# Second mixer of a fused decoder: the panels of the differential values ahead of the dilated queries and keys, and twelve half panels with the dilated rotary turns spread among the heads

## The reference

```
cq, ck, cv, dq, dk, dv = split_cols(h @ w_in, IN1_SPLITS)          # six times 512 columns
cq = apply_rope(cq, cos128, sin128) * DIL_DH ** -0.5               # dilated: 4 heads of 128
ck = apply_rope(ck, cos128, sin128)
o_c = dilated_attention(cq, ck, cv)
q1, q2 = apply_rope(dq[..., 0, :], ...), apply_rope(dq[..., 1, :], ...)   # differential: 4 heads, 2 x 64
k1, k2 = apply_rope(dk[..., 0, :], ...), apply_rope(dk[..., 1, :], ...)
o_d = differential_attention(q1, q2, k1, k2, dv, lam)              # softmax 1 - lam * softmax 2, times dv
o_d = rmsnorm(o_d, diff_norm) * (1.0 - lambda_init)
return concatenate([o_c, o_d]) @ w_out
```

## Time and profile before

| | |
|---|---|
| median of three runs | 1557.31 us |
| span of the profiled execution | 1554.0 us |
| what lies around the span, against that median | 3.3 us |
| PE busy | 1499.8 us, 97% |
| DVE busy | 1171.7 us, 75% |
| ACT busy | 763.9 us, 49% |
| chain that ended last: PE | 76% |
| chain that ended last: DVE, ACT | 13%, 7% |
| the mixer's stretch, from the first differential swap to the first matmul of `out1` | 778.81 to 861.12 us |

### The profile page before, as it was taken

One profiled execution on the slowest core, in us unless ns is written; L12 is line 12 of the kernel. 1 busy time (PEld: TensorE's weight loads), 2 busy tenths in 40 slices (PEclk: granted clock), 3 DMA queues, 4 the chain that ended last, 5 costly groups with the idle time before them and its releaser, 6 DMA issues.

```text
span 1554.0 us, 23910 instructions
## 1 busy us (share of the span) xinstructions
PE 1499.8 (97%) x9958; PEld 1343.8 (86%) x9958; DVE 1171.7 (75%) x1387; ACT 763.9 (49%) x935; POOL 94.1 (6%) x66
## 2 busy tenths in 40 slices
PE   7999999999999999999998899999999989999988
PEld 6888899988888888888887888888899869899967
DVE  7878668756887788787676688787779676579774
ACT  5333456445433453334445543345565675564662
POOL 2000010011000010000100100001113001003100
PEclk9999999999999999999999999999999999999999
DMA  7555535214655555555441365554344315444302
GB/s 272 209 190 189 170 131 188 82 55 159 213 189 199 179 178 190 190 185 194 163 163 56 134 216 190 192 188 175 151 163 152 109 42 189 175 149 152 120 28 81
DMA packets 51888, 246.76 MB, mean 159 GB/s; under 512 B 4619, under 2 KB 5771, under 8 KB 27718
## 3 DMA queue, kind: packets, MB, share of 16 engines
q1 hardware_dynamic: 50662, 238.29, 43.8%
q0 software_dynamic: 1120, 6.96, 1.2%
HBM read 244.18 MB, written 1.05 MB: 158 GB/s over the span
## 4 chain that ended last, share of the span: by engine, by line
PE 76%; DVE 13%; ACT 7%; issue 3%; DMA 0%; SPq 0%; DVEq 0%; ACTq 0%; POOL 0%
PE ps L1109 20%; PE ps L1111 10%; PE ps L1060 9%; PE ps L1062 9%; PE ps L1061 9%; PE ps L1162 8%; PE ps L1317 4%; PE ps L1163 4%; DVE w_lo L1890 3%; ACT w_hi L1571 2%; DVE act_two L1998 1%; PE ps L1465 1%; ACT work L1784 1%; ACT act_two L1649 1%; PE ps L1454 1%
## 5 line engine op out<-in xcount | busy, mean ns | idle before, releaser
L1571 ACT ACTIVATE w_hi<-raw 128x2048 fp32r<-128x2048 f32 x186 | 355.2, 1914 | 396.6 <-PE ps L1111 276.6
L1890 DVE TENSOR_TENSOR w_lo<-raw,w_hi 128x2048 fp32r<-128x2048 f32 x186 | 432.4, 2331 | 139.1 <-ACT w_hi L1571 136.3
L1109 PE MATMUL ps<-act_two,w_hi 128*128 128x512 f32 x1408 | 445.1, 398 | 5.0 <-DVE w_lo L1890 2.4
L1060 PE MATMUL ps<-act_two,w_hi 128*128 128x256 f32 x1120 | 329.0, 294 | 9.9 <-DVE act_two L1998 5.3
L1111 PEld LDWEIGHTS ps<-act_two,w_lo 128*128 128x128 f32 x1408 | 265.6, 189 | 63.1
L1061 PE MATMUL ps<-act_two,w_hi 128*128 128x256 f32 x1120 | 316.7, 283 | 0.0
L1062 PE MATMUL ps<-act_two,w_lo 128*128 128x256 f32 x1120 | 316.7, 283 | 0.0
L1111 PE MATMUL ps<-act_two,w_lo 128*128 128x256 f32 x1408 | 277.5, 279 | 0.0
L1060 PEld LDWEIGHTS ps<-act_two,w_hi 128*128 128x128 f32 x1120 | 214.6, 192 | 17.0 <-issue 6.1
L1109 PEld LDWEIGHTS ps<-act_two,w_hi 128*128 128x128 f32 x1408 | 215.5, 190 | 8.0 <-DVE w_lo L1890 3.6
L1061 PEld LDWEIGHTS ps<-act_two,w_hi 128*128 128x128 f32 x1120 | 214.7, 192 | 4.4 <-issue 4.3
(11 more groups left out here) (286 smaller groups left out, 1995.5 us busy)
## 6 DMA issues: line engine op xcount, KB each, us to landing
raw<-panels SPq DMA_DIRECT2D x184, 1024.0 KB, 4.8
raw<-panels SPq DMA_DIRECT2D x80, 512.0 KB, 4.9
raw<-panels SPq DMA_DIRECT2D x8, 256.0 KB, 5.7
table<-tab POOLq DMA_DIRECT2D x1, 1472.0 KB, 9.4
table<-tab POOLq DMA_DIRECT2D x1, 1216.0 KB, 5.5
xn<-x_in SPq DMA_DIRECT2D x4, 256.0 KB, 4.9
work<-mem_in POOLq DMA_DIRECT2D x1, 1024.0 KB, 9.3
xn<-mem_in POOLq DMA_DIRECT2D x1, 1024.0 KB, 6.3
```

The lines of the kernel that those rows point to most:

```text
L1060: pe.matmul(o, l[0], r[0], start=start, stop=False, skip_group_check=shared)
L1109: pe.matmul(grid(ps[:, bank + half], 2), w[half][0], act_two[:, slots[c]], start=c == 0, stop=False)
L1571: nc.scalar.activation(w_hi[:, s], raw[:, s], ACT.Copy).then_inc(panel_hi, 1)
L1890: tt(w_lo[:, s], raw[:, s], w_hi[:, s].bitcast(F32), ALU.subtract).then_inc(panel_lo, 1)
```

## The change

Four things change, all in the order of `in1` and its neighbours:

1. The two panels of the differential v come as panels 4 and 5, the dilated q and k as panels 6 to 9. The array of panels in memory stays as it was; SP takes them by a list, `IN1_SOURCE`. Transfers keep their number and size.
2. Only panels 4 and 5 stand whole among the differential turns. Their places become 0 and 2, so two swaps stand between them. Panels 6 to 11 are woven in as twelve halves, and two more splits are made by halves.
3. The four dilated turns move from two pairs (before the first and before the second head's scores) to rounds 1 and 2 (one each) and round 3 (two). They all use bank 3, so each swap waits for the rope just before it. Bank 3 was the second bank of `turn_p`; the differential heads now all turn in bank 2, and each of these waits for the copy of the head before.
4. The copy of panel 9 stands right behind its second half. The copies of the others stay behind the following round.

The last places of `BESIDE_1` are 4 and 5 for panel 11 before, and 5 and 6 after.

```
+AT_ONCE = [("act", "evacuate", ("in1", 9))]
...
             out.append(first)
+            if rest and rest[0] in AT_ONCE:
+                out.append(rest.pop(0))
...
-BESIDE_1 = [0, 0, 1, 1, 2, 3, 4, 5]
+BESIDE_1 = [0, 0, 0, 1, 1, 1, 2, 2, 3, 4, 5, 6]
+IN1_SOURCE = [0, 1, 2, 3, 8, 9, 4, 5, 6, 7, 10, 11]
...
-    out += weave(rounds(ROPE, [("r64b", g) for g in (0, 2, 1, 3)]), panel_list("in1", None, 4, 8), range(4))
-    ropes = [[(e, k, (("r128", g),)) for g in pair for e, k, _ in ROPE] for pair in ((0, 2), (1, 3))]
+    out += weave(rounds(ROPE, [("r64b", g) for g in (0, 2, 1, 3)]), panel_list("in1", None, 4, 6), [0, 2])
+    turns = [[]] + [[(e, k, (("r128", g),)) for e, k, _ in ROPE] for g in (0, 1)] + [[(e, k, (("r128", g),)) for g in (2, 3) for e, k, _ in ROPE]]
...
-    out += weave(merge(ropes, heads, [[]] * 7 + norms, [[]] * 9 + [[("dve", "gate_out", (("dil", 0),))]]),
-                 halves(panel_list("in1", None, 8)), BESIDE_1)
+    out += weave(merge(turns, heads, [[]] * 7 + norms, [[]] * 9 + [[("dve", "gate_out", (("dil", 0),))]]),
+                 halves(panel_list("in1", None, 6)), BESIDE_1)
...
-            ropes["r128", g] = (cqk[:, 2 * g:2 * g + 2], tab(2, "swap128"), tab(2, "cos128"), tab(2, "sin128"), 6 + g // 2,
-                                evac("in1", 4 + g))
+            ropes["r128", g] = (cqk[:, 2 * g:2 * g + 2], tab(2, "swap128"), tab(2, "cos128"), tab(2, "sin128"), 3,
+                                evac("in1", 6 + g))
...
+        def turn_bank(unit):
+
+            return 2 if unit[0] == "dif" else 2 + att_index[unit] % 2
...
+                    if b == BASE["in1"]:
+                        source = b + IN1_SOURCE[n - b]
...
-                if rope_index[unit] >= 2:
-                    pe.wait_ge(dve_done, at("dve", "rope", rope_list[rope_index[unit] - 2][0]))
+                ago = 1 if unit[0] == "r128" else 2
+                if rope_index[unit] >= ago:
+                    pe.wait_ge(dve_done, at("dve", "rope", rope_list[rope_index[unit] - ago][0]))
...
-                if i >= 2:
-                    pe.wait_ge(act_done, at("act", "p_cols", att_list[i - 2]))
-                p, bank = probs[:, i % 2, 0], ps[:, 2 + i % 2]
+                ago = 1 if unit[0] == "dif" or i and att_list[i - 1][0] == "dif" else 2
+                if i >= ago:
+                    pe.wait_ge(act_done, at("act", "p_cols", att_list[i - ago]))
+                p, bank = probs[:, i % 2, 0], ps[:, turn_bank(unit)]
```

More of the change, by code:

```diff
@@ L838, in build @@
             dest["in0", 12 + k] = (rows(rv, k), "rows", ACT.Copy)
-            dest["in1", 8 + k] = (rows(dv, k), "rows", ACT.Copy)
+            dest["in1", 4 + k] = (rows(dv, k), "rows", ACT.Copy)
             dest["in1", 10 + k] = (rows(cv, k), "rows", ACT.Copy)
@@ L850, in build @@
             dest["in1", k] = (blocks(dqk, k), "cols", ACT.Copy)
-            dest["in1", 4 + k] = (blocks(cqk, k), "cols", ACT.Copy)
+            dest["in1", 6 + k] = (blocks(cqk, k), "cols", ACT.Copy)
             for l in range(2):
@@ L1794, in p_cols @@
                 n = 512 if full else 384
-                nc.scalar.activation(p_t[:, i % 2, 0:n], ps[:, 2 + i % 2, 0:n], ACT.Copy).then_inc(act_done, 1)
+                nc.scalar.activation(p_t[:, i % 2, 0:n], ps[:, turn_bank(unit), 0:n], ACT.Copy).then_inc(act_done, 1)
             def y_hi(l, b):
```

## The result

The changed kernel takes 1561.97 us, the median of five runs (1560.21 to 1564.14), against 1557.31 us before. The ratio of the times is 1.0035, with a 95% interval of 1.0023 to 1.0046: slower by 4.7 us by the medians and by about 5.5 by the ratio. The profiled execution has a span of 1558.6 us, 4.6 more than before. One number shows where these lie: from the first differential swap to the first matmul of `out1` before took 861.12 - 778.81 = 82.3 us (the first start is in the table of times above), after it takes 864.90 - 778.03 = 86.9 us. The stretch is 4.6 us longer, and so is the span: in these two profiles nothing else changed in sum.

What follows compares the result with a forecast made beforehand. PE, busy 97% of the span, bounds the kernel, with 9.0 us of waits to win. Shift 1.2, clock 1.7 + 1.6 - 0.4 gave +4.1, the ledger +5.35; taken +4.2, so 1561.5 us, range 1557.0 to 1563.8.

Steps and rivals of the forecast that it cites:

- Nothing from the splits: Two more splits in halves on DVE: about 0.1 us each, beside PE's work, so nothing lost or won.
- Cause A: Swap of differential group 1, now right behind group 2's, waits for group 0's rope: about 2.1 us near 786.5.
- Cause B: Swap of dilated group 3 shares bank 3 with group 2's, so waits for its rope: 3.95 us at about 825.
- What goes: At the third head's later steps and after, to 849: PE's waits of 1.47, 0.82, 0.48, 0.86 and 0.23 us vanish.
- Cause C: First dilated output waits for panel 11's copy, now behind the last exponential and both squares: 4.1 us at about 850.
- The clock: Falls after Cause B (1.7 us) and Cause C (1.6), less 0.4 for low clock inside the wait; both falls 0.55.
- The forward walk: Start of `out1` followed step by step: 1.2 us later, plus clock 1.7 + 1.6 - 0.4, sum +4.1 us.
- the ledger: Count over the stretch to `out1`: waits 13.15 against 9.0, +4.15, clock 2.9 against 1.7, +1.2: +5.35 us.
- The 3.3 us: Added around the profiled span of 1558.2 us to bring it to the median: 1561.5 us.
- the clock falling once or not at all: Rival on the clock in the mixer: one fall 1560.0 us, chance 0.22; none 1558.5 us, chance 0.08.
- B and C were not covered: Rival: at 825 or 850, DVE or ACT finishes before PE needs it; one covered gives 1556.1 us, chance 0.10.
- the third rival: From last half panel to `out1`: spread halves outweigh waits if Cause B and Cause C both go; 1550.7 us, chance 0.05.

Runs made afterwards that it cites:

- the kernel with bank 7: Changed kernel with the last dilated turn (group 3) in bank 7 in place of bank 3; ratio to the kernel before 1.0021.
- the kernel with the copy moved: Changed kernel with the copy of panel 11 right behind its second half on ACT, ahead of the last exponential and both squares; ratio to the kernel before 1.0018.
- the idle matmuls: Changed kernel plus ten unread matmuls of constants, five before the swap of dilated group 3, five before the first dilated head's output; ratio to the kernel before 1.0024.
- the norm ahead: Norm's squares, sums and `cn_rstd` put before the heads: on the spread turns 0.9971, on the three undoings 0.9974, on the kernel before 0.9982, all against the kernel before.
- the three undoings: Changed kernel with panel 5 ahead of differential group 1's swap, dilated group 3 in bank 7, panel 11's copy at once; ratio to the kernel before 0.9981.
- the spread turns: The three undoings with dilated turns one, two, one over rounds 1 to 3, group 2 in bank 7, panel 8's copy at once; ratio to the kernel before 0.9987.
- panel 5 ahead: Changed kernel with panel 5 moved ahead of the swap of differential group 1; ratio to the kernel before 1.0029.

## Why the prediction was right

It named slower, 1561.5 us, and the median is 1561.97. Its steps one by one:

- *Nothing from the splits.* Right. No wait of PE in the changed kernel is ended by one.
- *Cause A.* Forecast 2.1 us, measured 2.10.
- *Cause B.* Forecast 3.95 us, measured 3.64. Counted from the first swap, PE was free 0.1 later than in my sum and the rope 0.2 earlier, half of that because the copy of panel 8 took 0.5 up to the next start and not 0.6. That the bank is the cause is shown by the kernel with bank 7.
- *What goes.* Right: none of the waits between 828 and 849 is left.
- *Cause C.* Forecast 4.1 us, measured 3.91. Shown by the kernel with the copy moved.
- *The clock.* Both falls came, with confidence only 0.55. The first was forecast at 1.7 and cost 1.65. The second was forecast at 1.6 and cost 2.5: this term was the one mis-sized. I had taken the fall of before as its length. It lasted twice as long here (an estimate from the granted clock in windows of 2 us: low for 6.8 us against 3.4). Part of it did lie inside the wait, as I had allowed for with 0.4, but 4.9 us of PE's work at 0.50 still came behind it.
- *The sum.* Forecast +4.2 on the stretch, measured +4.6. The forward walk came to +4.1, the ledger to +5.35. With measured terms the ledger is still too high: waits 2.10 + 3.64 + 3.91 + 1.22 + 1.48 = 12.35 less 9.0, and clock 4.15 less 1.6, make +5.9. The walk was the better sum. A likely reason: a wait in the rows starts when the last matmul's modelled end is over, 0.28 us after its start where its neighbours follow at 0.12, so each wait is some 0.16 us longer than shown, and the kernel before had ten of them, the changed one five. The kernel with the idle matmuls has a row in favour: a wait shown as 0.29 us made the way between two heads' scores 0.49 longer. Beside that, the first fall cost less over the whole stretch than right behind it, since 0.5 us of it would else have been a wait for DVE.
- *What cancelled.* The walk was close by some luck. From the swap of group 3 to the turn of the second dilated head it had 0.9 + 16.96 + 2.85 and 1.7 for the clock, 22.4 us, and 21.57 were measured (828.24 to 849.81): 0.8 too many. From the first dilated output to `cn_rstd` it had 0.65 + 1.95 and 1.6 for the clock, 4.2 us, and 5.26 were measured (854.22 to 859.48): 1.1 too few. The 0.4 taken off was too much as well. Swap 3 came 0.2 earlier. Together that makes the +4.6 in place of +4.1.
- *The span against the median.* The 3.3 us are not what lies around the span of one execution: the profiled execution of the changed kernel took 1560.51 us at a span of 1558.6, which is 1.9. They also hold the distance of a faster execution from the median. For the changed kernel the same difference is 1561.97 - 1558.6 = 3.4, so the 3.3 carried over, but by luck: it needed a profiled execution as much under its median as the one before must have been.

Of the rivals, the clock falling once or not at all did not come true in the profile, and B and C were not covered. With both covered by other edits, and the first wait gone too, the kernel is faster than before, as the third rival had it (0.9981). Its price of 1550.7 us is a ratio of 0.9957, and no kernel reached it: the lowest is 0.9971, with the norm ahead.

## What to carry to other kernels

When steps are moved, look for each one at what is queued ahead of the step that it waits for, on the other engine. Here the exchange of many waits of 0.2 to 1.5 us for three of 2 to 4 us lost time: the sum of the waits grew from 9.0 to 12.35 us, and two of the long ones cost the clock behind them as well. Two things that share a buffer and follow one another directly on the engine that is never to wait need two buffers, or work in between. And a wait that is mended alone may come back behind it: 1.74 of 3.64 us did here, so the edits have to be tried together. When the gain of an edit is read from a stretch of the profile, the stretch has to reach past the next place where the clock may fall: up to `out1` the three undoings won 3.9 us, and 1.5 of them were gone behind it.

## What was not expected of the hardware

The wait of 2.10 us at 786 is the same in the profiles of four kernels. In the profiles of the changed kernel and of that with the copy moved the clock stayed high behind it; in those with bank 7 and with the added matmuls it fell (0.59 over 4.2 us, 0.55 over 3.5 us). So a wait of 2 us costs 1.6 us more in some executions and nothing in others. The five runs of the changed kernel are in keeping with this, though they do not show where the clock fell: three between 1560.2 and 1562.0 us at a mean clock of 0.995, two at 1563.6 and 1564.1 at 0.994. The eleven of the spread turns, which have a wait of 2.90 us, part in the same way: eight between 1551.4 and 1555.1 us at 0.996 to 0.999, three between 1556.8 and 1557.2 at 0.995. One profile does not show the price of such a wait, and kernels with fewer waits of this size have less of it.

The waits of 1.22 and 1.48 us before `out1` behave alike. Two such waits (0.84 to 1.22 and 1.47 or 1.48 us) stand there in eight of the profiles. In five of them the clock fell, for 1.5 us; in three (the kernel before, the changed one, panel 5 ahead) it did not. In the three kernels with the norm ahead (0.95 or 0.97 and 0.86 or 0.88 us) it stayed high there.

Ten matmuls of constants in two waits kept the clock at 1.00, and their own 6.7 us of PE's time cost 0.2. Mending the waits was worth more: 103.0 against 109.6 us up to the feed-forward block.
